# Decoder trunk on one core: the feed-forward up projections as six products of 272 columns in place of five unequal ones

## The reference, cut to what matters

```python
def swiglu(x, w_in, w_out):
    gate, up = jnp.split(x @ w_in, 2, axis=-1)
    return (jax.nn.silu(gate) * up) @ w_out

x = x + mixer(rms_norm(x, norm_mix[i]))
x = x + swiglu(rms_norm(x, norm_ffn[i]), ffn_w_in[i], ffn_w_out[i])
```

## Time and profile before

| | us |
|---|---|
| median of three runs | 3189.87 |
| lowest and highest of them | 3188.98, 3190.84 |
| span of the profiled execution, first to last instruction | 3189.4 |
| TensorE busy in it | 3084.1 |
| VectorE busy | 1910.9 |
| ScalarE busy | 1107.8 |

### The profile page before, as it was taken

One profiled execution on the slowest core, in us unless ns is written; L12 is line 12 of the kernel. 1 busy time (PEld: TensorE's weight loads), 2 busy tenths in 40 slices (PEclk: granted clock), 3 DMA queues, 4 the chain that ended last, 5 costly groups with the idle time before them and its releaser, 6 DMA issues.

```text
span 3189.4 us, 76176 instructions
## 1 busy us (share of the span) xinstructions
PE 3084.1 (97%) x31972; PEld 2862.0 (90%) x31972; DVE 1910.9 (60%) x3366; ACT 1107.8 (35%) x1825; POOL 130.8 (4%) x247
## 2 busy tenths in 40 slices
PE   8999999999999999997998998999999999999998
PEld 7998999999887999997997777999999888899997
DVE  6777654556666554555547886653555767764454
ACT  4223322233555322222336665321233223332222
POOL 0000000001322000000000000000000000000000
PEclk9999999999999999999999999999999999999999
DMA  3322222233443222222220001222222222222222
GB/s 130 101 87 76 87 91 87 86 100 98 135 128 113 87 85 90 85 98 68 74 74 12 21 25 29 86 87 91 86 94 85 88 87 88 81 86 99 80 93 73
DMA packets 104594, 268.99 MB, mean 84 GB/s; under 512 B 12802, under 2 KB 45954, under 8 KB 104146
## 3 DMA queue, kind: packets, MB, share of 16 engines
q1 hardware_dynamic: 91346, 228.54, 21.9%
q0 software_dynamic: 13056, 37.64, 3.5%
HBM read 247.61 MB, written 18.52 MB: 83 GB/s over the span
## 4 chain that ended last, share of the span: by engine, by line
PE 83%; DVE 9%; ACT 3%; DVEq 3%; issue 2%; DMA 0%; SPq 0%; ACTq 0%
PE ps L650 21%; PE ps L659 14%; PE ps L661 9%; PE ps L662 9%; PE ps L663 9%; PE ps L660 7%; PE ps L1143 3%; PE ps L1121 2%; PE ps L743 1%; DVE cell L2468 1%; DVE arena_r L2114 1%; PE ps L808 1%; PE ps L1153 1%; PE ps L996 1%; DVEq L2084 1%
## 5 line engine op out<-in xcount | busy, mean ns | idle before, releaser
L650 PE MATMUL ps<-arena_r 128*128 128x272 f32 x6816 | 952.7, 296 | 40.9 <-DVE arena_r L2605 15.2
L650 PEld LDWEIGHTS ps<-arena_r 128*128 128x128 f32 x6816 | 884.7, 191 | 85.8 <-issue 55.6
L1565 ACT ACTIVATE arena_r<-ring 128x1024 fp32r<-128x1024 f32 (+1 forms) x240 | 275.2, 1147 | 832.8 <-PE ps L663 819.2
L659 PE MATMUL ps<-hb_r,arena_r 128*128 128x480 f32 x1408 | 536.4, 381 | 3.3 <-DVE arena_r L2139 3.0
L661 PE MATMUL ps<-hb_r,arena_r 128*128 128x304 f32 x1408 | 427.1, 303 | 0.0
L663 PE MATMUL ps<-hb_r,arena_r 128*128 128x304 f32 x1408 | 425.3, 302 | 0.0
L662 PE MATMUL ps<-hb_r,arena_r 128*128 128x304 f32 x1408 | 425.2, 302 | 0.0
L660 PE MATMUL ps<-hb_r,arena_r 128*128 128x240 f32 x1408 | 383.9, 273 | 0.0
L2139 DVE TENSOR_TENSOR arena_r<-ring,arena_r 128x1024 fp32r<-128x1024 f32 (+1 forms) x240 | 318.3, 1326 | 49.2 <-ACT arena_r L1565 49.1
L2168 DVE TENSOR_TENSOR arena<-ps,rstd 128x544 f32<-128x544 f32 x176 | 127.4, 724 | 332.0 <-PE ps L663 331.7
L661 PEld LDWEIGHTS ps<-hb_r,arena_r 128*128 128x128 f32 x1408 | 264.7, 188 | 41.5
(11 more groups left out here) (433 smaller groups left out, 4321.4 us busy)
## 6 DMA issues: line engine op xcount, KB each, us to landing
ring<-in_w_up SPq DMA_DIRECT2D x176, 512.0 KB, 3.4
ring<-in_w_mix SPq DMA_DIRECT2D x112, 512.0 KB, 3.5
ring<-in_w_down SPq DMA_DIRECT2D x64, 704.0 KB, 4.1
arena<-in_hg_s POOLq DMA_DIRECT2D x16, 512.0 KB, 3.8
out_hg_so<-arena POOLq DMA_DIRECT2D x16, 512.0 KB, 2.9
ring<-in_w_hgout SPq DMA_DIRECT2D x16, 512.0 KB, 3.5
arena<-in_cache_k SPq DMA_DIRECT2D x128, 64.0 KB, 1.9
arena<-in_cache_v POOLq DMA_DIRECT2D x128, 64.0 KB, 2.3
```

What stands on the lines that cost most here:

```text
L650: mm = pe.matmul(PS[:, 2 * a + hf, 0:HALF], part[:, ws], rhs[:, o:o + HALF], start=start and n == 0, stop=stop and n == 2)
L659: pe.matmul(both(a), wide, parts[:, :, c, 0:TA], start=start, stop=False, skip_group_check=True)
L1565: act.activation(wh[n % 2][:, 0:width], ring[:, k * SLOT:k * SLOT + width], ACT.Copy)\
```

## The change

In the up projections TensorE calls `block_product` with the layer's high and low input in place of `dual_product`, with the same wait for each input block, and `scaled` evicts both halves in one operation. The down projections and their eviction stay.

```diff
@@ TensorE, up(i, par) @@
                             first = begin and not s and par == 0
-                            product(2 * par + g, g, ff_h2, KC, "ff_hl" if first and not g else None, KC * layer)
+                            for c in range(KC):
+                                if first and not g:
+                                    pe.wait_ge(S("ff_hl"), KC * layer + c + 1)
+                                mm = block_product(2 * par + g, g, c, ff_hh, ff_hl, c == 0, c == KC - 1, wh, wl)
+                            mm.then_inc(S("unit_done"), 1)
@@ VectorE @@
             def scaled(dst, a):
-                dve.tensor_tensor(dst, main(a), rstd[:, :], ALU.mult)
-                dve.tensor_tensor(ff_side[a % 2], side(a), rstd[:, 0:TA], ALU.mult)
-                dve.drain()
-                return dve.tensor_tensor(dst[:, 0:TA], dst[:, 0:TA], ff_side[a % 2], ALU.add)
+                return dve.tensor_tensor(halves(dst), acc(a), halves(rstd[:, :]), ALU.mult)
```

## The result

The changed kernel takes 3197.92 us (median of eight runs, 3194.51 to 3203.34) against 3189.44 for the kernel before (eight runs, 3184.39 to 3192.40), a ratio of 1.0026, 95% interval [1.0016, 1.0037]. A second measurement of the unchanged pair gave 1.0025 [1.0013, 1.0036]. The profiled execution took 3194.88 us, 1.6 us of it around its span of 3193.3.

What follows compares the result with a forecast made beforehand. TensorE, busy 97% of the span, was taken to bound the kernel. 6.8 - 1.4 - 4.0 = +1.4 us took the span from 3189.4 to 3190.8; with 0.5 around it 3191.3 us, range 3184.5 to 3197.5.

Steps and rivals of the forecast that it cites:

- The down projections keep the five-product form: Down passes behind the up passes: code stays as it was, so no time was added for them, forecast difference 0.
- Hence +4.8 ns a step ... +6.8 us: TensorE, up projections: six products cost 751.5 ns a step against 746.7 for five, over 1408 steps, all on the path.
- The stall, -4.0 us: First up pass of each layer: TensorE's wait for the fifth product's weights goes, as shorter evictions let VectorE make them earlier.
- Layer 1's cadence, -1.4 us: Layer 1's first up pass: its last 141 steps, 9.9 ns slower than elsewhere, come to 751.5 ns like the others.
- VectorE: Up projections' evictions: one operation for three saves some 0.75 us, 176 times, about 130 us, worth nothing in second passes.
- Columns alone: TensorE, up loop: the sixth product is free since columns are equal; -5.4, 3184.5 us; chance 0.08.
- the stall stays: First up passes: another thing holds the fifth weights back and only the price is paid; +5.4, 3195.3 us; chance 0.10.
- The other rhythm: Up passes: the six-product loop settles into layer 1's slower cadence in every pass; +1.4 + 13.9, 3205 us; chance 0.08.
- The longer loop is fetched again: Up loops: the longer loop's start must be fetched at each of 24 branch returns; 18 us, 3209.5; chance 0.04.

Runs made afterwards that it cites:

- the padded kernels: The kernel before and the changed kernel, each with 64 unused bytes a partition between the up projections' inputs and weights: 3182.11 us and 3183.44 us.

## Why the prediction was wrong, by its steps

*"The down projections keep the five-product form."* That step failed, for +4.7 of the 6.6 us that the passes miss the forecast by. It took unchanged code for unchanged time. The two kernels with one product of the other form show what holds instead: a down pass runs at one of two steps, 746.7 or 753.3 ns, and the last up product ahead of it decides which. The new form, placed as here, leaves it at the longer one: 8 passes x 0.59 us.

*"Hence +4.8 ns a step ... +6.8 us."* The sign was right for these two placements, the size not: the step measured +6.6 to +6.7 ns, over 1408 steps +9.3 us. The reason given was wrong. The price came from the mixers' products, the same form but with weights and inputs at another distance. The runs with 32 and 64 bytes show that placement alone moves this form between 746.7 and 753.4 ns. So it isn't a price of a multiplication at all. The Trainium skill's fixed cost for each warm matmul ("TensorE: Matmul & The Clock Gate", "Wait — 56ns, not 53.3ns?"), which the prediction weighed against that row, isn't borne out either: padded, 176 multiplications more a pass take the same time to 0.01 us in second up passes.

*The stall, -4.0 us.* Right. The wait at the fifth product is gone from layer 0's first pass; L2144, the former L2139, ends at 388.28 after a stretch of VectorE as the prediction redrew it, in order of time:

```profile
382.88 1.36 DVE L2173 TENSOR_TENSOR arena<-ps,rstd 128x544 f32<-128x544 f32 x2
384.33 0.73 DVE L2205 TENSOR_TENSOR arena<-arena 128x544 f32<-128x544 f32 x1
385.78 0.72 DVE L2208 TENSOR_TENSOR arena_r<-arena,arena_r 128x544 fp32r<-128x544 f32 x1 [0.73 <-ACT arena_r L1617]
386.42 0.72 DVE L2173 TENSOR_TENSOR arena<-ps,rstd 128x544 f32<-128x544 f32 x1
387.06 1.22 DVE L2144 TENSOR_TENSOR arena_r<-ring,arena_r 128x1024 fp32r<-128x1024 f32 x1
```

Two evictions in 1.36 us, then product, low half, third eviction and weights, each where it was put in the order. Its worth: 4.2 us with VectorE's work put back, 4.5 between the padded kernels, and 4.6 as what is left here of +3.3 - 9.3 + 1.4. All three lie a little above the 4.0 that the prediction took for the most.

*Layer 1's cadence, -1.4 us.* Right in this pair (134.87 to 133.51, against +0.04 in layer 2), but for a reason the text had only guessed: no first pass of the six-part form in any run settled at 756.6 ns, while in the old form the place wanders between executions. It was worth 1.4 us in the two profiled executions of the kernel before without a pad, in another layer each time. That it was one pass, and 1.4 us, is luck of the execution: the old form with the small multiplication had three such first passes, the padded one none.

*VectorE.* 111 us less in place of 130: an eviction saves 0.63 (111.1/176), as the old operations overlapped in part; in the second passes that was worth nothing, as forecast.

*Rivals.* "Columns alone" (3184.5) and "the stall stays" (3195.3) fall in this pair, though the first describes the padded pair. "The other rhythm" (3205) was the family that took place, but at 753.4 and not 756.6 ns, and it missed that the down passes would follow. Its price was also summed wrongly: 13.9 us is what 756.6 ns costs above the old 746.7, so it stands in place of the 6.8 and not on top of it, and the rival comes to 13.9 - 1.4 - 4.0 = +8.5, 3198.4 us. That this is near the measured 3197.92 is luck, since 4.7 of the measured loss is in the down passes. "The longer loop is fetched again" falls: no gaps inside the passes, and 156 packets of instructions for the 151 of this row of the kernel before:

```profile
q8 instruction: 151, 2.47, 0.3%
```

The sum of the steps as measured, 9.3 - 1.4 - 4.6 + 4.7 = +8.0, leaves 0.5 of the medians' 8.5, within the spread of the rest.

What stays open: why 0, 32 and 64 bytes give 753.4, 750.0 and 746.7 ns in second up passes; no other distances were tried beside the exchange of the two halves. It is also open by what the end of an up pass sets the step of the down pass, and why the mixers gain only in part.

## What to carry to other kernels

Price a form of multiplication from rows whose weights and inputs lie as they will lie, and compare all stretches after a change pass by pass, the untouched code behind it above all. Where two forms of equal columns on a full TensorE differ by under 1% a step, it is worth trying to move one operand by 64 bytes before the form is dropped: here that turned +0.26% into -0.19%, against a kernel before without the 64 bytes.

## What was not expected of the hardware

- At the full granted clock and with TensorE busy throughout, the same six multiplications of 272 columns ran at 753.4, 750.0 or 746.7 ns a step in second up passes, with 0, 32 or 64 bytes put between the input and the weights. Another order of the weights gave 751.6, and the old form 746.7 or 756.6. No up or down pass settled below 746.7.
- One product of 6 us in the other form set the next 66 us, in all eight passes of either kernel. The down passes behind it know two steps, 746.7 and 753.3 ns, and don't copy the one ahead: 756.6 was followed by 746.7, and 750.0 by 746.7.
- A small multiplication between the two passes turned this round: 753.3 ns followed up passes that ended at 746.7 (five of five), and 746.7 ns those that ended at 753.4 (eight of eight) or 756.6 (three of three).
